# A hybrid attention, retention and expert step: the attention scores' fifth product over 128 rows instead of 64

## The reference

```python
q = (rms_norm(cq, q_norm_w) @ w_uq).reshape(B, S, 4, 192)
q = rms_norm(q, q_head_norm_w)
kv = (ckv @ w_ukv).reshape(B, S, 4, 128 + 128)
k = rms_norm(concat([kv[..., :128], broadcast(krope)]), k_head_norm_w)
# latent tokens: q, k = rope_2d(q), rope_2d(k); keys and values of the cached context in front
s = einsum('bqhd,bkhd->bhqk', qblk, k) * 192 ** -0.5     # blocks of 128 queries
o = einsum('bhqk,bkhv->bqhv', softmax(s), v)
```

## Time and profile before

| what | us |
|---|---|
| three timed runs, median (lowest to highest) | 3787.43 (3781.59 to 3791.14) |
| the profiled execution, whole | 3788.99 |
| its span on the core | 3787.2 |
| mean granted clock of TensorE in it | 0.953 of full |

### The profile page before, as it was taken

One profiled execution on the slowest core, in us unless ns is written; L12 is line 12 of the kernel. 1 busy time (PEld: TensorE's weight loads), 2 busy tenths in 40 slices (PEclk: granted clock), 3 DMA queues, 4 the chain that ended last, 5 costly groups with the idle time before them and its releaser, 6 DMA issues.

```text
span 3787.2 us, 55805 instructions
## 1 busy us (share of the span) xinstructions
PE 3508.8 (93%) x18342; PEld 2928.4 (77%) x18342; DVE 3123.3 (82%) x6003; ACT 1283.5 (34%) x1810; POOL 1694.9 (45%) x1067
## 2 busy tenths in 40 slices
PE   6899889978999917899999999999999999999998
PEld 2899767767444415789888888889889999999997
DVE  7455668864499969899999999989898888888888
ACT  6411443333222217433333333323222332323322
POOL 1232110032122220255555555555577777777774
PEclk9999989989999955799999999999999999999999
DMA  8599329964110024799999999999899999999997
GB/s 294 198 350 350 128 87 331 350 226 140 37 42 33 28 100 190 252 341 338 349 341 339 341 334 344 337 366 345 300 365 366 346 332 348 332 345 336 338 343 249
DMA packets 403105, 1033.24 MB, mean 273 GB/s; under 512 B 30826, under 2 KB 193422, under 8 KB 395442
## 3 DMA queue, kind: packets, MB, share of 16 engines
q1 hardware_dynamic: 229516, 493.89, 37.7%
q0 software_dynamic: 128880, 486.07, 35.1%
q10 hardware_dynamic: 44600, 52.06, 3.9%
HBM read 883.74 MB, written 148.16 MB: 272 GB/s over the span
## 4 chain that ended last, share of the span: by engine, by line
PE 34%; DVE 15%; DMA 7%; issue 6%; POOL 1%; ACT 0%; DVEq 0%; SPq 0%; ACTq 0%; POOLq 0%
PE p_y L2474 17%; DVE rows L2367 6%; DMA rows<-u_rows,pairsT 6%; PE p_a L2462 6%; PE p_a L2459 6%; PE p_a L2458 6%; DVE u_lo L2342 2%; DVE v_lo L2349 2%; DVE hot_w L2053 1%; POOL rows L2279 1%; DVE pairsT L2355 1%; DVE g_hi L2358 1%; DMA rows<-in_v,pairsT 1%; DVE hot_j L2049 1%; DMA w_ring<-weights_spill 0%
## 5 line engine op out<-in xcount | busy, mean ns | idle before, releaser
L2279 POOL DMA_INDIRECT rows<-in_v,pairsT x384 | 742.6, 1934 | 289.0 <-DVE h_rows L2380 194.1
L2279 POOL DMA_INDIRECT rows<-u_rows,pairsT x384 | 594.1, 1547 | 493.1 <-DVE pairsT L2367 422.2
L2458 PE MATMUL p_a<-h_hi,u_hi 128*128 128x384 f32 x2048 | 687.9, 336 | 4.1 <-DVE h_lo L2421 2.4
L2459 PE MATMUL p_a<-h_lo,u_hi 128*128 128x384 f32 x2048 | 691.6, 338 | 0.0
L2241 ACT ACTIVATE v_hi<-v_raw 128x1024 fp32r<-128x1024 f32 x256 | 272.0, 1062 | 746.9 <-PE p_y L2474 740.1
L2367 DVE CUSTOM_DVE_ANT_0 rows<-rows,h_rows 128x1024 f32<-128x1024 f32 x384 | 451.7, 1220 | 59.4 <-DMA rows<-u_rows,pairsT 59.4
L2474 PE MATMUL p_y<-v_hi,g_hi 128*128 128x512 f32 x1536 | 488.8, 399 | 7.7 <-DVE g_hi L2358 7.2
L2380 DVE SCALAR_TENSOR_TENSOR h_rows<-rows,pairsT,h_rows 128x1024 f32<-128x1024 f32 x381 | 467.7, 1279 | 16.5 <-DMA rows<-in_v,pairsT 16.4
L2474 PE MATMUL p_y<-v_lo,g_hi 128*128 128x512 f32 x1536 | 478.2, 392 | 0.0
L2462 PE MATMUL p_a<-h_hi,u_lo 128*128 128x384 f32 x2048 | 401.1, 337 | 22.2 <-DVE u_lo L2342 22.2
L2458 PEld LDWEIGHTS p_a<-h_hi,u_hi 128*128 128x128 f32 x2048 | 385.6, 188 | 15.1 <-issue 4.6
(11 more groups left out here) (353 smaller groups left out, 5574.5 us busy)
## 6 DMA issues: line engine op xcount, KB each, us to landing
u_raw<-in_uT SPq DMA_DIRECT2D x256, 512.0 KB, 7.8
v_raw<-in_v SPq DMA_DIRECT2D x256, 512.0 KB, 6.5
w_ring<-weights_spill POOLq DMA_DIRECT2D x32, 1536.0 KB, 14.4
key_cols<-in_uT SPq DMA_DIRECT2D x64, 512.0 KB, 6.9
u_rows<-key_rows SPq DMA_DIRECT2D x64, 512.0 KB, 5.9
wada<-in_w_ada SPq DMA_DIRECT2D x24, 1024.0 KB, 7.0
u_rows<-pairsT ACTq DMA_DIRECT2D x48, 512.0 KB, 6.6
weights_spill<-wt SPq DMA_DIRECT2D x24, 1024.0 KB, 3.9
```

Of the source, the lines that this page charges most:

```text
L2279: pool.indirect_dma_start(rows[s][n % SLOTS][:], None, (keep.u_rows, v_rows)[g], at).then_inc(rows_in[s][n % SLOTS], 16)
L2458: nc.tensor.matmul(p_a[:, 0:GT], u_hi[s][:, k, :], h_hi[:, k, :], start=k == 0, stop=False)
L2459: nc.tensor.matmul(p_a[:, 0:GT], u_hi[s][:, k, :], h_lo[:, k, :], start=False, stop=False)
```

## The change

Blocks 12 and 13 of `q_halves`, shared by two heads each, become blocks 12 to 15, one for each head. A head's rotary remainder stands in its own 64 partitions and the other 64 partitions of its block are zero. The fifth product reads all 128 partitions of the block and of `k_rope`. Nothing else of the sum changes, since the rows added are multiplied by zero. ACT writes the four blocks with two instructions of 64 partitions instead of one of 128; POOL writes the zeros once into both buffers at the start of `stage_qkv`; the stored tile grows from 896 KB to 1 MB. The two buffers grow by 1 KB per partition each; in exchange a 1 KB buffer (`ckvT0`) and the throw-away output of two ACT squares move into space that other tiles have then free.

```diff
@@ -672,17 +672,18 @@
     st = [m.sb(f"qst{i}", [P, 8]) for i in range(4)]
     hst = [m.sb(f"hst{i}", [P, 3, 8]) for i in range(2)]
     cqT_hi, cqT_lo = ([m.sb(f"cqT_{x}{i}", [P, 4, P], F32R) for i in range(2)] for x in ("hi", "lo"))
-    ckvT = [m.sb(f"ckvT{i}", [P, 2, P]) for i in range(2)]
     qs = [m.sb(f"qs{i}", [P, HEADS, QK]) for i in range(2)]
     ks = m.sb("ks", [P, HEADS, NOPE])
     k_rows, q_rows = m.sb("k_rows", [P, 2, 2, 2 * ROPE], F32R), m.sb("q_rows", [P, HEADS, 2, ROPE], F32R)
     scratch = keep.pairsT[:].rearrange("p r t -> p (r t)")
-    sizes = {"q_sq": HEADS * QK, "k_sq": HEADS * NOPE, "z_sq": Z_ATT, "m1": HEADS * ROPE, "m2": HEADS * ROPE,
+    sizes = {"q_sq": HEADS * QK, "k_sq": HEADS * NOPE, "z_sq": Q_RANK + ROPE, "ckvT": KV_RANK, "m1": HEADS * ROPE, "m2": HEADS * ROPE,
              "qr": HEADS * ROPE, "kr": HEADS * ROPE, "ckvn": KV_RANK}
     starts = dict(zip(sizes, itertools.accumulate(sizes.values(), initial=0)))
-    q_sq, k_sq, z_junk, m1, m2, qr, kr, ckvn = (scratch[:, starts[x]:starts[x] + sizes[x]] for x in sizes)
+    q_sq, k_sq, z_junk, first_ckvT, m1, m2, qr, kr, ckvn = (scratch[:, starts[x]:starts[x] + sizes[x]] for x in sizes)
+    ckvT = [first_ckvT.rearrange("p (a k) -> p a k", a=2), m.sb("ckvT1", [P, 2, P])[:]]
     by_head = lambda x: x.rearrange("p (h c) -> p h c", h=HEADS)
     ALL = TILES + 1
+    kv_junk = keep.kn_hi[:, 0:2, CTX * P:ALL * P]
     km = keep.mix[:].rearrange("p t c -> p (t c)")[:, ALL * Z_ATT:ALL * (Z_ATT + ROPE)].rearrange("p (t c) -> p t c", c=ROPE)
     km_temps = [keep.early_v[:].rearrange("p t c -> p (t c)")[:, i * ALL * ROPE:(i + 1) * ALL * ROPE].rearrange("p (t c) -> p t c", c=ROPE)
                 for i in range(3)]
@@ -704,7 +705,7 @@
     kr_ready, k_split, k_rows_full, q_split, q_rows_full = (sem(x) for x in ("kr_ready", "k_split", "k_rows_full", "q_split", "q_rows_full"))
     kn_hi_kept, kn_lo_kept, k_rope_kept, qn_hi_kept, qn_lo_kept, q_rope_kept, rest_kept = (
         sem(x) for x in ("kn_hi_kept", "kn_lo_kept", "k_rope_kept", "qn_hi_kept", "qn_lo_kept", "q_rope_kept", "rest_kept"))
-    q_out = [sem(f"q_out{i}") for i in range(2)]
+    q_out, zeros_full = [sem(f"q_out{i}") for i in range(2)], sem("zeros_full")
     km_done, cache_out = sem("km_done"), sem("cache_out")
 
     with nc.Block() as block:
@@ -716,6 +717,7 @@
             sp.dma_start(a["out"][3][0, 0], keep.z1[:, 0, Q_RANK + KV_RANK:Z_ATT]).then_inc(cache_out, 16)
             sp.wait_ge(ckvn_full, 1)
             sp.dma_start(a["out"][2][0, 0], ckvn).then_inc(cache_out, 16)
+            sp.wait_ge(zeros_full, 1)
             for t in range(TILES - 2):
                 for kept in (qn_hi_kept, qn_lo_kept, q_rope_kept, rest_kept):
                     sp.wait_ge(kept, t + 1)
@@ -747,6 +749,11 @@
                 pool.wait_ge(q_split, t + 1)
                 nc.gpsimd.tensor_sub(by_head(q_rest), by_head(qr), q_rows[:, :, 0].bitcast(F32)).then_inc(q_rows_full, 1)
 
+            for half in keep.q_halves:
+                for b, other in enumerate((slice(ROPE, 2 * ROPE), slice(0, ROPE))):
+                    last = nc.gpsimd.memset(half[other, 12 + b:16:2].bitcast(F32), 0.0)
+            last.then_inc(zeros_full, 1)
+            pool.wait_ge(zeros_full, 1)
             for t in range(ALL):
                 key_rows(t)
                 query_rows(t)
@@ -761,8 +768,8 @@
                     act.wait_ge(head_sum, t - 3)
                 if t != CTX:
                     nc.scalar.activation(z_junk[:, 0:Q_RANK], z[:, 0:Q_RANK], ACT.Square, scale=Q_RANK ** -0.5, accum_out=s[:, 0:1])
-                    nc.scalar.activation(z_junk[:, Q_RANK:Q_RANK + KV_RANK], z[:, Q_RANK:Q_RANK + KV_RANK], ACT.Square, scale=KV_RANK ** -0.5, accum_out=s[:, 1:2])
-                nc.scalar.activation(z_junk[:, Q_RANK + KV_RANK:Z_ATT], z[:, Q_RANK + KV_RANK:Z_ATT], ACT.Square, scale=QK ** -0.5, accum_out=s[:, 2:3]).then_inc(z_squares, 1)
+                    nc.scalar.activation(kv_junk, z[:, Q_RANK:Q_RANK + KV_RANK].rearrange("p (a k) -> p a k", a=2), ACT.Square, scale=KV_RANK ** -0.5, accum_out=s[:, 1:2])
+                nc.scalar.activation(z_junk[:, Q_RANK:Q_RANK + ROPE], z[:, Q_RANK + KV_RANK:Z_ATT], ACT.Square, scale=QK ** -0.5, accum_out=s[:, 2:3]).then_inc(z_squares, 1)
                 act.wait_ge(z_squares, t + 1)
                 if t != CTX:
                     nc.scalar.activation(s[:, 3:5], s[:, 0:2], ACT.Sqrt, bias=keep.cols[:, 4:5]).then_inc(z_rms, 1)
@@ -817,7 +824,9 @@
                 if t < 0:
                     return
                 act.wait_ge(rest_full, t + 1)
-                nc.scalar.activation(keep.q_halves[t % 2][:, 12:14], pf[1][:, 0:2], ACT.Copy).then_inc(rest_kept, 1)
+                for b, own in enumerate((slice(0, ROPE), slice(ROPE, 2 * ROPE))):
+                    last = nc.scalar.activation(keep.q_halves[t % 2][own, 12 + b:16:2], pf[1][own, 0:2], ACT.Copy)
+                last.then_inc(rest_kept, 1)
 
             statistics(0)
             statistics(1)
@@ -860,7 +869,7 @@
                 dve.wait_ge(zT_full, t + 1)
                 if t >= 2:
                     dve.wait_ge(kv_full, t - 1)
-                nc.vector.tensor_copy(ckvT[t % 2][:], pckv[:, 0:KV_RANK].rearrange("p (k t) -> p k t", k=2)).then_inc(ckvT_full, 1)
+                nc.vector.tensor_copy(ckvT[t % 2], pckv[:, 0:KV_RANK].rearrange("p (k t) -> p k t", k=2)).then_inc(ckvT_full, 1)
                 if t == CTX:
                     return
                 dve.wait_ge(cq_hi_full, t + 1)
@@ -1107,7 +1116,7 @@
                 wait_count(pe, p_full, n - 1)
                 if t < TILES - 2:
                     pe.wait_ge(q_in[t % 2], (TILES - 1 - t) // 2 * 16 if t else 16 * (TILES // 2))
-                q, own = keep.q_halves[t % 2], slice((h % 2) * ROPE, (h % 2 + 1) * ROPE)
+                q = keep.q_halves[t % 2]
                 for b in cuts:
                     if b and not whole(n):
                         continue
@@ -1118,7 +1127,7 @@
                     nc.tensor.matmul(out, q[:, h], keep.kn_lo[:, h, keys], start=False, stop=False)
                     nc.tensor.matmul(out, q[:, 4 + h], keep.kn_hi[:, h, keys], start=False, stop=False)
                     nc.tensor.matmul(out, q[:, 8 + h], keep.k_rope[:, h, keys], start=False, stop=False)
-                    last = nc.tensor.matmul(out, q[own, 12 + h // 2], keep.k_rope[own, h, keys], start=False, stop=True)
+                    last = nc.tensor.matmul(out, q[:, 12 + h], keep.k_rope[:, h, keys], start=False, stop=True)
                     if b == 2 or not whole(n):
                         last.then_inc(s_full, 1)
 
@@ -2537,7 +2546,7 @@
         keep.w_in_in = [stack.enter_context(nc.semaphore(f"w_in_in{c}")) for c in range(2)]
 
         keep.gate_dram = nc.dram_tensor("gate_rows", [2, 2, D], F32).ap()
-        keep.q_dram = nc.dram_tensor("q_halves", [TILES - 2, P, 14, P], F32).ap()
+        keep.q_dram = nc.dram_tensor("q_halves", [TILES - 2, P, 16, P], F32).ap()
         keep.gate_out = stack.enter_context(nc.semaphore("gate_out"))
         keep.uq_in, keep.norms_in = stack.enter_context(nc.semaphore("uq_in")), stack.enter_context(nc.semaphore("norms_in"))
         keep.w_out_in = stack.enter_context(nc.semaphore("w_out_in"))
@@ -2570,7 +2579,7 @@
                 return
             with ExitStack() as s2:
                 m2 = Mem(nc, s2)
-                keep.q_halves = [m2.sb(f"q_halves{i}", [P, 14, P], F32R) for i in range(2)]
+                keep.q_halves = [m2.sb(f"q_halves{i}", [P, 16, P], F32R) for i in range(2)]
                 keep.kn_hi, keep.kn_lo, keep.k_rope = (m2.sb(x, [P, HEADS, T + P], F32R) for x in ("kn_hi", "kn_lo", "k_rope"))
                 keep.early_v = m2.sb("early_v", [P, 4, HEADS * P])
                 keep.v = [keep.early_v[:, t] for t in range(4)] + [late_v[:, t] for t in range(6)]
```

## The result

| | before | after |
|---|---|---|
| timed runs, median (lowest to highest), us | 3786.76 (3781.59 to 3791.14), 4 runs | 3755.11 (3748.94 to 3759.36), 4 runs |
| profiled execution, its span, us | 3788.99, 3787.2 | 3759.21, 3756.8 |
| mean granted clock of TensorE | 0.953 | 0.953 |
| first score product, us from the span's start | 544.0 | 547.4 |
| third maximum | 563.61 | 561.40 |

The changed kernel is faster: the ratio of the medians is 0.9921 (95% interval 0.9903 to 0.9938), 31.65 us saved. So the direction and the place were right and the size was not. 28.6 us of the saving are the attention itself, its stage from here on.

What follows compares the result with a forecast made beforehand. PE was taken to bound the attention stage. Steps 20.5 plus start 4.5, less queues 2.4 and ACT's copies 1.1, saved 21.5 us: 3766 us median, own range 3758 to 3773, 8-in-10 range 3757 to 3778.

Steps and rivals of the forecast that it cites:

- The late starts: PE in the attention stage: without the 64-row product the third cut falls from 1.27 to 0.87 us, a step by 1.0.
- The rival that the change does nothing: Late starts come from reading the same `k_rope` columns twice or closing the PSUM sum, not rows: 3789 us; 5 in 100.
- The ring: Attention steps: a chain of waits through DVE, ACT and PE becomes the bound, 12.55 us over two steps, 6.28 a step.
- small latencies: Allowance in the chain through DVE, ACT and PE over two attention steps: 12.4 us taken as 12.55.
- the nineteen ordinary steps: Attention steps after the start: some twenty ordinary ones save 0.76 us each, 15 us.
- the three pairs with three transposes: Three attention steps where DVE has three transposes, each with the step behind it: 1.0 us saved a pair, 3 us.
- the last steps: End of the attention stage, four short steps among them and six without transposes: 2.5 us saved.
- The start: First cuts of the attention stage, at the lower clock: third maximum 4.5 us earlier, bounds 2 and 6.
- The queues: DMA in the attention stage: about 367 GB/s under higher demand, a loss of 2.4 us, bounds 0 and 12.
- The rival on the queues: DMA queues bind the attention stage at 350 GB/s, losing 10 to 14 us: 3775 us; 20 in 100.
- ACT's copies: ACT's second copy in each of nine tiles makes DVE wait: a loss of 1.1 us, bounds 0 and 3.5.
- The clock: Rival: PE idles in attention steps and its clock falls to 1.2 GHz, 25 us slower, 3812 us; 4 in 100.

Runs made afterwards that it cites:

- third experiment: Kernel before, with the 64-row fifth products of the second and third cut put next to each other behind the eight 128-row products: 3771.31 us (one run).
- first: Changed kernel, keeping the new 16-block layout but with the fifth product again over the head's own 64 rows: 3786.91 us (10 runs), ratio 0.9999.
- second: Kernel before, old 14-block layout, with the fifth product over all 128 rows and the other head's remainder not zeroed: 3752.57 us (4 runs), ratio 0.9915.

## Why the prediction was wrong in size, step by step

**The late starts.** Right: the third cut measured 0.87, forecast 0.87; the second 0.96, forecast 0.95. The third experiment ties them to the change into and out of 64 rows. The rival that the change does nothing is out by the first and second: in the second and in the changed kernel the fourth and fifth product read the same columns of `k_rope` and the fifth closes the sum, as before, and no start is late.

**The new bound.** The ring was right by name, place and pattern, and mis-sized: 6.28 a step forecast, 6.14 measured, with 6.04 and 6.18 us in turn where 6.1 and 6.5 were forecast. Two things were off. The three parts came out a little shorter: maximum to turn 3.90 (forecast 3.93), turn to scaled output 1.76 + 2.45 = 4.21 (4.28), scaled output to maximum 4.17 (4.22), 0.15 together. And I had added 0.12 for "small latencies" that the measured parts already contained. 0.27 over two steps is 0.14 a step, and twenty times that 2.8 us. From the third maximum to the end the stage took 232.4 us before and 209.4 after: 23.0 us saved, 20.5 forecast, 2.5 more. Maximum by maximum, the step behind the third gave 1.8 (8.10 to 6.25, as it had the low clock before), the nineteen ordinary steps 17.5 or 0.92 each (forecast 0.76), the three pairs with three transposes 2.6 (forecast 3), the last steps 1.1 (forecast 2.5). So the ordinary steps were missed by more than the 2.5, and the last steps, with two falls of the clock after and one before, gave some of it back.

**The start.** Forecast 4.5 us (bounds 2 to 6), measured 5.6, and 5.8 in the run with the new rows at the start alone. I had counted four cuts at the low clock and a part of the fall at 559. The clock instead rose 2.7 us sooner, and the fall at 559 was gone: 1.1 us more. How much of the start's gain is the late starts at the low clock and how much the clock's own course, no run here separates.

**The queues.** Forecast a loss of 2.4 us at 367 GB/s, measured none at 386. Of the terms this is the one that was wrong in itself; in the others the mechanism held and the size was off. The loss did not follow from its own sum: 67.1 MB at 367 GB/s take 183 us, less than the 187 there were, so the term should have been nothing even at that rate, and at 345 GB/s, 194.5 us, it is 7.5 and not 12. And the rate was too low. I chose a rate below the row of full load (385) because its neighbour at share 1.01 had 331; but the changed kernel carries 373 GB/s over 173 us at a share of 1.05, so the 331 was what was asked of the queues and no limit. The higher row was the one to take. The rival on the queues, 20 in 100, is out by the run with small loads; the run without transposes shows where it would begin.

**ACT's copies.** Forecast 1.1 us, measured none that shows. DVE does wait a little for ACT's later split, but gives it back elsewhere. The waits of DVE from 440 to 530 us, after:

```profile
DVE cqT_lo L877 <- ACT cqT_hi L784: 1.6, 6, 0.3
...
DVE hst L912 <- ACT pairsT L802: 0.9, 3, 0.3
```

and before:

```profile
DVE hst L903 <- ACT pairsT L795: 2.5, 8, 0.3
```

The new wait of 1.6 us stands in the earlier trace rows's place as forecast; the old one shrank by the same 1.6.

**What remains.** 1.1 + 2.5 + 2.4 + 1.1 = 7.1 of the 10.1 us between forecast and result. The last 3 lie outside the stage. In the two profiles the first score came 3.4 us later after, 1.9 of it in the projection, and the part behind the stage, with the same instructions, was 5.2 us shorter; the rest is between the profiles and the medians. Over the twelve profiled kernels the part behind ranges from 2979.9 to 2991.2 us. The six with all rows full have a mean of 2983.1 and the six with 64-row products 2986.9, but the two groups overlap, from 2982.6 to 2988.8, and before is the longest of all. The interval on the saving, 23.5 to 36.7 us, holds the stage's 28.6 alone as well as 31.65. I leave it open.

**The range.** All four terms of the sum erred to one side, as each was taken from its cautious side: padding in the ring, the slower DMA row, the fewer slow cuts, a cost for the copies. The good ends that the range used, 0.85 us a step, start 6, no loss to queues or copies, give 1.8 + 1.5 + 2.4 + 1.1 = 6.8 us under 3766. But 0.85 was no bound of the step: PE's own 1.0 was. With 6.04 us a step the first term is 20 x 0.24 = 4.8, the sum 9.8, and 3756; with 3 us for the scatter of a profile and of the medians the range should have begun at 3753. The gain measured is 7.04 - 6.14 = 0.90 a step.

**The clock.** Right not to weigh it: 1.00 from 562 to 735 us after. It fell in the last steps alone, to 0.91 on average from 735 to 771; over the whole stage it was 0.97 after and 0.96 before, above the 0.95 that the forecast had named as a sign of being wrong.

## What to carry to other kernels

In a run of matmuls over all 128 rows, one over 64 rows makes its neighbours late: pad its weights with zeros, or put several such products next to each other so that the change is paid once. When a bound goes, sum the next ring from its measured parts with nothing added, take a queue's limit from the stretch where it was loaded fully, and charge a loss only where the sum of bytes over rate gives one. The last steps of this stage held the clock low for a different time in each kernel, so compare stages step by step and not by their length alone. A saving at the start of a stage can be worth more than its instructions, since it may decide when the clock rises.

## What the runs showed of the hardware

- A product of 384 columns over 64 rows between ones over 128: its start 0.10 us late, the one after it 0.20 late, and about 0.10 on the following cut's first; 0.40 us in all at 2.4 GHz. At 1.2 GHz a cut took 2.20 us against 1.6 to 1.7.
- Two such products side by side: starts 0.27, 0.28 and 0.26 us apart, where full ones have 0.175; 0.17 us more in all than one alone, so one payment for both.
- The clock rose 4.5 to 5.3 us after the first score without such changes at the start, 5.3 with them paired, 8.0 to 15.6 us with one in every cut, though PE's busy share was 0.98 (14.75 of 15 us) there. Busy time in the profile does not show the late starts: the products' ends are modelled.
- The queues kept 386 GB/s for 160 us in mixed loads and stores of mostly 1 KB packets, while a DMA share of 1.01 stood for 331 GB/s before and one of 1.05 for 373 after: the share alone did not tell how much room was left.
